# A ring of weight slots in a decoder trunk: three slots with separate low halves, or four with the low half over the raw weights

## The chip, the cores and the metric

One NeuronCore of a Trainium2 chip. The metric is the device time of one launch in microseconds, the median of several runs. Engines: TensorE (PE in the profile) multiplies, VectorE (DVE) and ScalarE (ACT) work on tiles in on-chip memory (SBUF) or in the accumulator banks (PSUM), GpSimd (POOL) does a little elementwise work, and SyncE (SP) issues the DMAs. Each engine runs its own instructions in order; semaphores tie them together.

## The reference

Two decoder layers on 512 tokens of width 1024, all in float32. Cut to what matters here:

```python
for i in range(2):
    p = h @ w_in[i]                       # in0: 22 column tiles of 128, in1: 29
    mix = mixers(p) @ w_out[i]            # RWKV-7 and RG-LRU in layer 0, Conformer conv and Mamba-2 in layer 1
    h = layer_norm(alpha * h + mix)
    q, k, v = h @ wq[i], mem @ wk[i], mem @ wv[i]   # mem has 256 tokens
    h = layer_norm(alpha * h + softmax(q @ k.T / 16) @ v @ wo[i])
    h = layer_norm(alpha * h + square(relu(h @ w1[i])) @ w2[i])   # 4096 hidden
```

All the weight matrices come from HBM once: 263 chunks of 128 x 1024 floats (512 KB).

## The kernel before, in words

**Three products for one.** A float32 product is made of three passes: each operand is split into a rounded high half and the rest, its low half. `mm3` (L525) multiplies activation low by weight high (L527), high by low (L528), high by high (L529); for token-major stages the operands change sides, so L527 holds the weight's low half. A chunk is 24 multiplies of 512 columns in most stages, 24 of 256 columns in the `k` stages, 12 of 512 in the `v` stages.

**The ring of weight slots.** Chunk c uses slot c mod `W_SLOTS` (3) of three arrays: `w_raw`, `w_hi`, `w_lo`. SyncE loads `w_raw` (L339), after `w_split >= c - 2`, that is, when VectorE has made the low half of chunk c-3. ScalarE's `split` (L1055) waits for the landing and for `chunk_done >= c - 2` (TensorE is through with chunk c-3), and copies `w_raw` to `w_hi` (L1063). VectorE's `split` (L1506) waits for that and subtracts into `w_lo` (L1512), which counts up `w_split`. TensorE waits for `w_split >= c + 1` before it starts chunk c, and counts up `chunk_done` at its end.

**Where the splits stand.** The splits are written into the instruction order of ScalarE and VectorE by hand. In a loop over the chunks of a stage both call `chunk(stage, i)`: split up to chunk c + `W_SLOTS` - 1, then wait for `chunk_done` of c, then do the work on chunk c's output. `ahead` does the same without that last wait. So when chunk c-1 is done, both engines split chunk c+2 and only then turn to what follows. Between stages stand calls such as `split(FIRST["out0"] + 2 + W_SLOTS)` (L1231, L1775) before the mixer's output is turned back to features (L1234), `split(FIRST["wo0"] + W_SLOTS)` (L1289, L1891) before the softmax (`row_max`, `probs`), and those in `ln_std` (L1240) and `residual` (L1819) inside the LayerNorms after `out0` and `out1`.

**Stages, in order, per layer l.** `in` (22 or 29 chunks), the mixer, `out` (8 or 12), `k`, transposes of h to features (`to_features`, L952), `v`, `q`, attention, `wo`, transposes, four times `up` and `down` (8 chunks each), transposes. `out`, `v`, `wo` and `down` run in two halves of output columns; the last chunk (or two, `by_token`) of a half goes token tile by token tile, and VectorE's `residual` adds each tile to h. In `in0` and `in1` the vector work of the mixers is woven into the chunk loop; `in1` has 77 filter taps (L1528) on VectorE, beside sums on GpSimd. SyncE's order also has x (`h`, 2 MB) behind a wait at chunk `out0`+2, six loads of LayerNorm rows (`gb`, 1 MB) and two of mem (1 MB).

Of the kernel before, what the change touches and what calls it, by code (L numbers as in the profile page):

```python
# [14 lines left out]
F32R = mybir.dt.float32r  # L15
# [4 lines left out]
P = 128  # L20
# [4 lines left out]
MEM = 256  # L25
HALF = 512
CHUNK = 1024
W_SLOTS = 3
PAD = 4
PW = PAD + T  # L30
ALPHA = 4.0 ** 0.25
# [30 lines left out]
FIRST = {}  # L62
# [78 lines left out]
def build(nc, x_tok, x_feat, mem_feat, weights, vectors, lora, lru_w, ln_rows, out):  # L141
    with ExitStack() as ctx:
        base = (nc.sbuf_base + 31) // 32 * 32
        place = {"at": base}

        def sb(name, shape, dt=F32, at=None):

            size = 4
            for n in shape[1:]:
                size *= n  # L150
            if at is None:
                at = place["at"]
                place["at"] = at + (size + 31) // 32 * 32
            return nc.alloc_sbuf_tensor_at(name, shape, dt, offset=at)

        w_raw = sb("w_raw", [P, W_SLOTS, CHUNK])
        w_hi = sb("w_hi", [P, W_SLOTS, CHUNK], F32R)
        w_lo = sb("w_lo", [P, W_SLOTS, CHUNK], F32R)
        h_at = place["at"]
        h = sb("h", [P, NT, D])  # L160
        act_at = place["at"]
# [126 lines left out]
        def S(name):  # L288
            if name not in sems:
                sems[name] = ctx.enter_context(nc.semaphore(name))  # L290
            return sems[name]
# [19 lines left out]

        landed = [S(f"w_landed{i}") for i in range(W_SLOTS)]
        block = ctx.enter_context(nc.Block())
# [10 lines left out]
        @block.sync  # L324
        def _(sp):
            sp.dma_start(stage[:, 0:2], x_feat[:, 0:2]).then_inc(S("x_in0"), 16)
            sp.dma_start(w_raw[:, 0], weights[0]).then_inc(landed[0], 16)
            for i in range(1, 4):
                sp.dma_start(stage[:, 2 * i:2 * i + 2], x_feat[:, 2 * i:2 * i + 2]).then_inc(S(f"x_in{i}"), 16)
            sp.dma_start(w_raw[:, 1], weights[1]).then_inc(landed[1], 16)  # L330
            sp.dma_start(vec[:], vectors).then_inc(S("vec_in"), 16)
            sp.dma_start(lora_sb[:], lora).then_inc(S("const_in"), 16)
            sp.dma_start(lru_sb[:], lru_w).then_inc(S("const_in"), 16)
            ln_at = {FIRST["out0"] + 6: 0, FIRST["up0_0"] + 2: 1, FIRST["down0_3"] + 1: 2,
                     FIRST["out1"] + 3: 3, FIRST["up1_0"] + 2: 4, FIRST["down1_3"] + 1: 5}
            for c in range(2, N_CHUNKS):
                if c >= W_SLOTS:
                    sp.wait_ge(S("w_split"), c - W_SLOTS + 1)
                sp.dma_start(w_raw[:, c % W_SLOTS], weights[c]).then_inc(landed[c % W_SLOTS], 16)  # L339
                if c == FIRST["out0"] + 2:  # L340
                    sp.wait_ge(S("rst_mm"), 2 * NRC - 2)
                    sp.dma_start(h[:], x_tok).then_inc(S("h_in"), 16)
                if c in ln_at:
                    n = ln_at[c]
                    if n == 0:
                        sp.wait_ge(S("mix_done"), 1)
                    if n:
                        sp.wait_ge(S("h_ready"), NT * n)
                    if n == 3:
                        sp.wait_ge(S("s_bc"), 4)  # L350
                        sp.wait_ge(S("s_conv"), 8)
                    sp.dma_start(gb[:], ln_rows[n:n + 1].to_broadcast([P, 2, D])).then_inc(S("gb_in"), 16)
                for l in range(2):
                    if c == FIRST[f"out{l}"] + 6:
                        sp.wait_ge(S("mix_done"), l + 1)
                        sp.dma_start(stage[:].rearrange("p a t -> p (a t)")[:, 0:8 * MEM], mem_feat)\
                            .then_inc(S("mem_in"), 16)
            for t in range(NT):
                sp.wait_ge(S("out_rows"), t + 1)
                sp.dma_start(out[:, t], h[:, t]).then_inc(S("stored"), 16)  # L360
            sp.wait_ge(S("stored"), 16 * NT)
# [1877 lines left out]
```

## Time and profile before

| | |
|---|---|
| median of 3 runs | 1891.06 us (1889.82 to 1892.39) |
| the profiled execution | 1890.95 us, of it 1889.2 from the first to the last instruction |
| mean granted clock of TensorE | 0.942 |
| busy: TensorE, VectorE, ScalarE, GpSimd | 1718.4, 1127.0, 748.6, 214.2 us |
| the chain that ended last | TensorE 72%, VectorE 20%, ScalarE 4% |
| DMA | 155.53 MB, mean 82 GB/s |

How to read it: the times are one execution's. A busy TensorE is not one at its peak, since multiplies overlap; a 512-column multiply shows 0.39 us and the next starts 0.23 us later. The timeline gives, for each instruction, its start and length, and in brackets how long its engine sat idle before it and whose end released it. Where two rows of one engine are merged, the count follows the x.

### The profile page before, as it was taken

What the parts mean: (1) busy time and instruction counts of PE and PEld (TensorE: products, weight loads), DVE (VectorE), ACT (ScalarE), POOL (GpSimd) and SP (SyncE); (2) the same over time, 40 slices, a digit from 0 to 9 for tenths busy, and PEclk for the clock granted to TensorE, in tenths of its full rate; (3) what the DMA queues carried; (4) which work ended last, traced back from release to release, by engine and by line L of the source; (5) the groups of instructions that cost most, each with busy time, mean ns of one, the idle gap of its engine ahead of it and who ended that gap; (6) DMA issues with size and microseconds to landing.
All of it is one profiled execution on the core that took longest, in us unless ns stands there. A gap on an engine that the chain in (4) does not pass through costs nothing.

```text
span 1889.2 us, 26635 instructions
## 1 busy us (share of the span) xinstructions
PE 1718.4 (91%) x10894; PEld 1420.7 (75%) x10894; DVE 1127.0 (60%) x1377; ACT 748.6 (40%) x995; POOL 214.2 (11%) x186
## 2 busy tenths in 40 slices
PE   7996999889899999999996876789898999999997
PEld 6775899687777888888785664458887778888885
DVE  3689462555656543434559987886555665434345
ACT  4553431345425232324335554553454252324131
POOL 5112300000000000000006833440000000000000
PEclk9997995899999999999998888889998999999999
DMA  5220000444113333333231222003441223333331
GB/s 183 78 73 17 3 5 8 160 123 134 56 62 94 102 90 101 91 102 120 78 96 40 66 67 89 1 1 112 123 134 57 78 78 101 93 102 96 101 120 59
DMA packets 40873, 155.53 MB, mean 82 GB/s; under 512 B 4528, under 2 KB 4656, under 8 KB 39600
## 3 DMA queue, kind: packets, MB, share of 16 engines
q1 hardware_dynamic: 40752, 153.83, 26.4%
q8 instruction: 86, 1.41, 0.3%
q14 instruction: 35, 0.29, 0.1%
HBM read 151.72 MB, written 2.10 MB: 81 GB/s over the span
## 4 chain that ended last, share of the span: by engine, by line
PE 72%; DVE 20%; ACT 4%; issue 2%; DMA 0%; SPq 0%; POOL 0%; DVEq 0%; ACTq 0%; POOLq 0%
PE bank L527 21%; PE bank L528 21%; PE bank L529 21%; DVE cacc L1528 4%; DVE w_lo L1512 3%; DVE p L1525 1%; DVE sconv L1528 1%; DVE h L1528 1%; PE bank L685 1%; DVE nbh L1573 1%; ACT w_hi L1063 1%; PE bank L655 1%; PE bank L704 1%; PE bank L698 1%; DVE lnst L1834 1%
## 5 line engine op out<-in xcount | busy, mean ns | idle before, releaser
L1512 DVE TENSOR_TENSOR w_lo<-w_raw,w_hi 128x1024 fp32r<-128x1024 f32 x263 | 335.2, 1275 | 307.3 <-ACT w_hi L1063 304.7
L527 PE MATMUL bank<-act_lo,w_hi 128*128 128x512 f32 x1048 | 421.5, 402 | 55.7 <-DVE w_lo L1512 47.4
L1063 ACT ACTIVATE w_hi<-w_raw 128x1024 fp32r<-128x1024 f32 x263 | 279.0, 1061 | 367.7 <-PE bank L529 355.7
L528 PE MATMUL bank<-act_hi,w_lo 128*128 128x512 f32 x1048 | 416.7, 398 | 0.0
L529 PE MATMUL bank<-act_hi,w_hi 128*128 128x512 f32 x1048 | 415.7, 397 | 0.0
L527 PEld LDWEIGHTS bank<-act_lo,w_hi 128*128 128x128 f32 x1048 | 202.4, 193 | 107.2 <-issue 49.3
L529 PEld LDWEIGHTS bank<-act_hi,w_hi 128*128 128x128 f32 x1048 | 202.1, 193 | 43.6
L528 PEld LDWEIGHTS bank<-act_hi,w_lo 128*128 128x128 f32 x1048 | 202.7, 193 | 42.6 <-issue 0.7
L527 PE MATMUL bank<-w_lo,aux_hi 128*128 128x512 f32 x576 | 224.5, 390 | 5.3 <-DVE act_lo L1525 5.3
L528 PE MATMUL bank<-w_hi,aux_lo 128*128 128x512 f32 x576 | 224.1, 389 | 0.0
L529 PE MATMUL bank<-w_hi,aux_hi 128*128 128x512 f32 x576 | 224.1, 389 | 0.0
L484 POOL TENSOR_TENSOR cacc<-cacc,gtmp 128x512 f32<-128x512 f32 x44 | 73.5, 1671 | 664.6 <-ACT gtmp L1350 661.7
L527 PEld LDWEIGHTS bank<-w_lo,aux_hi 128*128 128x128 f32 x576 | 108.1, 188 | 28.9 <-DVE act_lo L1525 5.7
L527 PE MATMUL bank<-w_lo,act_hi 128*128 128x512 f32 x288 | 115.7, 402 | 12.8 <-DVE act_lo L1525 10.4
L529 PEld LDWEIGHTS bank<-w_hi,aux_hi 128*128 128x128 f32 x576 | 108.1, 188 | 22.5
L528 PEld LDWEIGHTS bank<-w_hi,aux_lo 128*128 128x128 f32 x576 | 108.1, 188 | 22.3
L528 PE MATMUL bank<-w_hi,act_lo 128*128 128x512 f32 x288 | 114.3, 397 | 0.0
L529 PE MATMUL bank<-w_hi,act_hi 128*128 128x512 f32 x288 | 114.2, 396 | 0.0
L1525 DVE TENSOR_TENSOR stage<-stage 128x512 f32<-128x512 f32 x64 | 44.3, 692 | 108.4 <-ACT stage L1321 108.4
L1321 ACT ACTIVATE stage<-bank 128x512 f32<-128x512 f32 x64 | 38.2, 597 | 146.1 <-PE bank L529 146.1
L1528 DVE SCALAR_TENSOR_TENSOR cacc<-cu,vec,cacc 128x512 f32<-128x512 f32 x75 | 91.7, 1278 | 0.0
L1525 DVE TENSOR_TENSOR aux_lo<-stage,aux_hi 128x512 fp32r<-128x512 f32 (+1 forms) x66 | 48.9, 741 | 59.8 <-ACT aux_hi L1323 53.7
(356 smaller groups left out, 2365.0 us busy)
## 6 DMA issues: line engine op xcount, KB each, us to landing
w_raw<-weights SPq DMA_DIRECT2D x263, 512.0 KB, 3.6
gb<-ln_rows SPq DMA_DIRECT2D x6, 1024.0 KB, 5.7
stage<-x_feat SPq DMA_DIRECT2D x4, 512.0 KB, 6.2
h<-x_tok SPq DMA_DIRECT2D x1, 2048.0 KB, 8.1
stage<-mem_feat SPq DMA_DIRECT2D x2, 1024.0 KB, 5.7
out<-h SPq DMA_DIRECT2D x4, 512.0 KB, 2.6
lora_sb<-lora SPq DMA_DIRECT2D x1, 512.0 KB, 8.8
lru_sb<-lru_w SPq DMA_DIRECT2D x1, 512.0 KB, 9.6
```

Source lines behind the costliest of these rows:

```text
L484: pool.tensor_tensor(acc, acc, gtmp[:, n % 2], ALU.add).then_inc(S("c_conv3"), 1)
L527: pe.matmul(o, whi, xlo, start=first, stop=False)
L528: pe.matmul(o, wlo, xhi, start=False, stop=False)
L529: return pe.matmul(o, whi, xhi, start=False, stop=last)
L655: last = pe.matmul(o[rows_(c), split_cols(j, c)], lhs[feat, j, cf], rhs[feat, j, cf], start=True, stop=True)
L685: last = each(lambda c, q, tok, feat, cf, ct: pe.matmul(compact(o, j, c, q, n), M_[b][tok, j, ct], halves(XT_[b][tok, j, ct], n, False), s ...
L698: last = each(lambda c, q, tok, feat, cf, ct: pe.matmul(compact(o, j, c, q, n), y_[tok, j, ct], halves(x_[tok, j, ct], n, True), start=Tru ...
L1063: act.activation(w_hi[:, s], w_raw[:, s], ACT.Copy).then_inc(S("w_hi_done"), 1)
L1321: done(act.activation(stage[:, n % 2], bank(f"up{l}_{q}", i)[:], ACT.Relu), "up_out")
L1512: dve.tensor_tensor(w_lo[:, s], w_raw[:, s], f(w_hi[:, s]), ALU.subtract).then_inc(S("w_split"), 1)
L1525: return dve.tensor_tensor(o, a, b_, op)
L1528: return dve.scalar_tensor_tensor(out=o, in0=a, scalar=s, in1=b_, op0=op0, op1=op1)
```

## The change

The low half of a chunk is written over its raw weights: `w_lo` gets the address of `w_raw`. The memory saved gives a fourth slot. The raw load of chunk c now waits for `chunk_done >= c - 3`, the end of TensorE's work on chunk c-4, since TensorE reads the low half from there; before, it waited for a split. `W_SLOTS` also stands in all the calls above, so each asks for one chunk more. The load of x keeps its place right behind the last chunk of that sort (`out0`+3 now).

```diff
--- before.py
+++ after.py
@@ -25,7 +25,7 @@
 MEM = 256
 HALF = 512
 CHUNK = 1024
-W_SLOTS = 3
+W_SLOTS = 4
 PAD = 4
 PW = PAD + T
 ALPHA = 4.0 ** 0.25
@@ -153,9 +153,10 @@
                 place["at"] = at + (size + 31) // 32 * 32
             return nc.alloc_sbuf_tensor_at(name, shape, dt, offset=at)
 
+        raw_at = place["at"]
         w_raw = sb("w_raw", [P, W_SLOTS, CHUNK])
+        w_lo = sb("w_lo", [P, W_SLOTS, CHUNK], F32R, at=raw_at)
         w_hi = sb("w_hi", [P, W_SLOTS, CHUNK], F32R)
-        w_lo = sb("w_lo", [P, W_SLOTS, CHUNK], F32R)
         h_at = place["at"]
         h = sb("h", [P, NT, D])
         act_at = place["at"]
@@ -335,9 +336,9 @@
                      FIRST["out1"] + 3: 3, FIRST["up1_0"] + 2: 4, FIRST["down1_3"] + 1: 5}
             for c in range(2, N_CHUNKS):
                 if c >= W_SLOTS:
-                    sp.wait_ge(S("w_split"), c - W_SLOTS + 1)
+                    sp.wait_ge(S("chunk_done"), c - W_SLOTS + 1)
                 sp.dma_start(w_raw[:, c % W_SLOTS], weights[c]).then_inc(landed[c % W_SLOTS], 16)
-                if c == FIRST["out0"] + 2:
+                if c == FIRST["out0"] + W_SLOTS - 1:
                     sp.wait_ge(S("rst_mm"), 2 * NRC - 2)
                     sp.dma_start(h[:], x_tok).then_inc(S("h_in"), 16)
                 if c in ln_at:
```

## Rows read from the trace of the kernel before

**Rows 1.** The page's groups: line, engine, count, then busy us, mean ns, idle before.
```profile
L1512 DVE TENSOR_TENSOR w_lo<-w_raw,w_hi 128x1024 fp32r<-128x1024 f32 x263 | 335.2, 1275 | 307.3 <-ACT w_hi L1063 304.7
...
L1063 ACT ACTIVATE w_hi<-w_raw 128x1024 fp32r<-128x1024 f32 x263 | 279.0, 1061 | 367.7 <-PE bank L529 355.7
```

**Rows 2.** VectorE timeline, in1: start us, us, what, [idle before].
```profile
982.86 1.23 DVE L1512 TENSOR_TENSOR w_lo<-w_raw,w_hi 128x1024 fp32r<-128x1024 f32 x1 [3.08 <-ACT w_hi L1063]
...
988.30 1.23 DVE L1512 TENSOR_TENSOR w_lo<-w_raw,w_hi 128x1024 fp32r<-128x1024 f32 x1 [3.08 <-ACT w_hi L1063]
```

**Rows 3.** Waits of TensorE, window 930 to 1170 (in1).
```profile
PE bank L527 <- DVE w_lo L1512: 32.4, 8, 7.9
```

**Rows 4.** Waits of TensorE, window 20 to 175 (in0).
```profile
PE bank L527 <- DVE w_lo L1512: 3.9, 4, 1.5
```

**Rows 5.** Windows view, in1: length, then busy PE, PEld, DVE, ACT, POOL, clock.
```profile
1002.00:1025.00 23.00, 13.69 (x52) 10.54 (x51) 23.00 (x17) 11.95 (x16) 17.77 (x11) 0.85 0.16 46
```

**Rows 6.** Waits of VectorE, window 976 to 1170.
```profile
DVE w_lo L1512 <- ACT w_hi L1063: 19.7, 5, 6.2
```

**Rows 7.** The page's DMA issues: count, KB each, median us from issue to landing.
```profile
w_raw<-weights SPq DMA_DIRECT2D x263, 512.0 KB, 3.6
```

**Rows 8.** Timeline of ScalarE at the end of k0.
```profile
418.17 0.38 ACT L1076 ACTIVATE k_hi<-bank 128x256 fp32r<-128x256 f32 x1 [1.40 <-PE bank L529]
...
421.05 0.38 ACT L1076 ACTIVATE k_hi<-bank 128x256 fp32r<-128x256 f32 x1 [1.41 <-PE bank L529]
```

**Rows 9.** Timeline of VectorE in in0.
```profile
83.59 1.23 DVE L1512 TENSOR_TENSOR w_lo<-w_raw,w_hi 128x1024 fp32r<-128x1024 f32 x1 [8.80 <-ACT w_hi L1063]
...
119.08 1.22 DVE L1512 TENSOR_TENSOR w_lo<-w_raw,w_hi 128x1024 fp32r<-128x1024 f32 x1 [4.89 <-ACT w_hi L1063]
```

**Rows 10.** Timeline of ScalarE in out0.
```profile
346.25 1.06 ACT L1063 ACTIVATE w_hi<-w_raw 128x1024 fp32r<-128x1024 f32 x1 [4.36 <-PE bank L529]
...
347.22 3.19 ACT L1234 ACTIVATE p<-bank,vec 128x512 f32<-128x512 f32 x4
```

**Rows 11.** Timeline of TensorE in out0.
```profile
352.22 0.77 PE L527 MATMUL bank<-w_lo,act_hi 128*128 128x512 f32 x1 [4.32 <-DVE act_lo L1525]
```

**Rows 12.** Windows view, 352 to 356; granted clock after the busy times.
```profile
352.00:356.00 4.00, 3.78 (x9) 3.03 (x10) 3.80 (x7) 0.90 (x3) 0.00 (x0) 0.50 0.00 0
```

**Rows 13.** Timeline of VectorE at the end of out0's first half.
```profile
361.96 1.23 DVE L1512 TENSOR_TENSOR w_lo<-w_raw,w_hi 128x1024 fp32r<-128x1024 f32 x1 [4.54 <-ACT w_hi L1063]
...
363.10 0.68 DVE L1528 SCALAR_TENSOR_TENSOR h<-h,bank 128x512 f32<-128x512 f32 x1
```

**Rows 14.** Timeline of TensorE in k0, then in k1.
```profile
404.90 0.35 PE L527 MATMUL bank<-aux_lo,w_hi 128*128 128x256 f32 x1 [4.45 <-DVE w_lo L1512]
...
1346.94 0.35 PE L527 MATMUL bank<-aux_lo,w_hi 128*128 128x256 f32 x1 [2.26 <-DVE w_lo L1512]
```

**Rows 15.** TensorE timeline, end of k0 (L963 transposes h).
```profile
422.02 2.95 PE L963 MATMUL bank<-ident,h 128*128 128x128 f32 x25 [0.24 <-DVE k_lo L1525]
```

**Rows 16.** Raw loads issued from 405 to 425, tile w_raw.
```profile
DMA to landing us min/median/max: 3.6/4.0/4.5
```

**Rows 17.** Timeline of ScalarE after q0.
```profile
494.13 1.06 ACT L1063 ACTIVATE w_hi<-w_raw 128x1024 fp32r<-128x1024 f32 x1
```

**Rows 18.** Timeline of VectorE after q0 (softmax).
```profile
496.69 0.69 DVE L1895 TENSOR_REDUCE small<-bank 128x2 f32<-128x512 f32 x1 [0.17 <-PE bank L529]
...
498.19 0.69 DVE L1895 TENSOR_REDUCE small<-bank 128x2 f32<-128x512 f32 x1 [0.61 <-PE bank L529]
```

**Rows 19.** Timeline of VectorE at the LayerNorm after wo0.
```profile
565.45 1.23 DVE L1512 TENSOR_TENSOR w_lo<-w_raw,w_hi 128x1024 fp32r<-128x1024 f32 x1 [3.23 <-ACT w_hi L1063]
...
566.93 0.69 DVE L1528 SCALAR_TENSOR_TENSOR h<-h,bank 128x512 f32<-128x512 f32 x1 [0.25 <-PE bank L529]
...
575.16 0.69 DVE L1528 SCALAR_TENSOR_TENSOR h<-h,bank 128x512 f32<-128x512 f32 x1 [0.67 <-PE bank L529]
...
577.05 0.16 DVE L1528 SCALAR_TENSOR_TENSOR lnmv<-lnmv,lnsd 128x1 f32<-128x1 f32 x1
```

## The prediction

> **What bounds the kernel now.** I read the page's groups first, then the waits by engine and by window, then the timelines at each place where TensorE stops. TensorE is the bound in most stages: splitting a chunk costs ScalarE 1.06 and VectorE 1.2 us [rows 1], and a 512-column chunk takes TensorE 5.44 us (VectorE's two splits in [rows 2] each follow a chunk's end and are 5.44 apart; that is 24 multiplies, one each 0.23 us). So in `q`, `wo`, `up` and `down` the ring of three slots is no limit. TensorE is held up by the weight split for 32.4 us in `in1` [rows 3] and for 3.9 in `in0` [rows 4]. That looks like the prize of a fourth slot, but in `in1` VectorE is busy for all 23 us of a 23 us window while TensorE works 13.7 [rows 5]. VectorE waits 19.7 us between 976 and 1170 [rows 6], and three of its five waits (3.08 us each [rows 2] shows one) come before the filter taps start. What is behind the stage is VectorE's own work; TensorE's stalls are what it leaves over.
>
> **The change part by part.** In steady state the new rule is harmless. The end of chunk c-1 now issues the raw load of chunk c+3. It lands 3.6 us later [rows 7], then come 1.06 and 1.23 us of splitting, with some 0.15 us of signals: the split stands 6.05 us after that end, and TensorE wants it 3 x 5.44 = 16.3 us after it (3 x 2.88 = 8.6 in `k`, by the two chunk ends in [rows 8]). The old split stood 2.5 us after the end, because its raw data lay there long before. The price is elsewhere: ScalarE and VectorE are in order and the split stands at a fixed place in their programs. Whatever follows it starts up to 3.65 us later, if the split came right after a chunk's end. In the loops of `up`, `q` and `down` nothing hangs on that: both engines finish the split at 6.05 us, the next output comes at 5.44, and the lag of 0.6 us stays inside the slack before `down` reads it. I take 0 there. If that cover failed, each of the 64 `up` chunks could cost 0.6. The serial places remain:
>
> 1. `in0`: TensorE stalls four times for a split, 3.9 us [rows 4]. VectorE's waits of 8.80 and 4.89 us [rows 9] end when ScalarE has its gate values, which come out of TensorE after chunks 9 and 15, both stalled for some 1.1 us. Splits one chunk ahead free both: -2.2. The first loads are not late: chunk 4's now waits for chunk 0, but is needed three chunks later.
>
> 2. `out0`, before the mixer's output goes back: ScalarE splits `out0`+4 right at the end of `out0`+1 (346.25) and only then turns the mixer rows back (347.22) [rows 10], and TensorE waits for their low halves until 352.22 [rows 11]. Now it must split `out0`+5, whose load starts at that same end. +3.7 (3.6 and 0.1 of signals), nothing hides it.
>
> 3. `out0`, end of the first half: VectorE splits at 361.96, then adds the four tiles from 363.10 [rows 13], and the second half needs the banks they free. The split now ends 3.5 later. +3.5.
>
> 4. `k0`, `k1`: TensorE waits 4.45 us for chunk `k0`+3 and 2.26 for `k1`+3 [rows 14], because that split stands behind the LayerNorm in both programs. With four slots the one that stands there is +4, wanted 2.88 us later; but the split inside `residual` waits for a load that the last `out` chunk releases. In layer 0 the split of mem already covers most of the first such wait, so the LayerNorm ends 1.4 later: 4.45 + 1.4 - 2.9 = 2.95, -1.5. In layer 1 nothing covers it, 3.5 later: +0.6.
>
> 5. End of `k` (2 times): chunk `k0`+7 ends at 421.0 [rows 8] and the transposes go on at 422.02, held by the last low half of k by 0.24 [rows 15]. Before that low half now stands the split of `v0`+2, whose load waits for the end of `k0`+6. Loads here take 4.0 [rows 16]: 4.0 + 1.06 + 1.23 + 0.42 + 0.2 after that end is 4.0 after the end of `k0`+7 against 1.0 now. +3.0 each, 6.0.
>
> 6. Softmax (2 times): the split of `wo0`+2 (494.13) [rows 17] stands before the loop over score tiles; VectorE starts it with waits of only 0.17 and 0.61 us for TensorE [rows 18] and then sets its pace, and TensorE waits at its end. The split of `wo0`+3 needs a load released by the last `q` chunk: 3.1 later, less those two waits and some overlap, +2.4 each, 4.8.
>
> 7. LayerNorm after `wo0`, `down0_3`, `wo1` (3 times): the last split before it starts at 565.45, the first tile at 566.93, 0.25 after it was free to; the last tile comes at 575.16 and takes until 577.2 [rows 19]. Starting 3.2 later at 2.05 us a tile against TensorE's 2.72, VectorE is 0.7 behind at the last tile: +0.65 each, 2.0. The split of `up`+1, which now stands earlier, lies beside the transposes, so its move gains 0. After `down1_3` no chunk is left to load: 0.
>
> 8. `in1`: at chunk 8 VectorE splits at 988.30 [rows 2] and then begins the taps that fill it to the end. Its split now waits for the load that chunk 7's end releases. ScalarE's copy of chunk 7 (some 0.65 us) stood before the split and now runs beside the load: 3.65 - 0.65 = +3.0. Later waits for the split hang on VectorE's own earlier steps (ScalarE's dt chain, the dt transposes), so they stay. Bounds: from -10 (the last two waits of [rows 6] go) to +6.
>
> Writing over its own input is free for VectorE: `h<-h,bank` does it in 0.68 for 512 columns [rows 13], half of the 1.23 of a 1024-column split; no row shows the new form, so bounds of 0 and 0.1 us, hidden except in `in1`. SyncE issues in order: behind a raw load that waits for TensorE now stand x, the LayerNorm rows and mem, all needed over 15 us later: 0.
>
> Sum: -2.2 + 3.7 + 3.5 - 1.5 + 0.6 + 6.0 + 4.8 + 2.0 + 3.0 = +19.9. Against the profiled execution's 1890.95 us that is 1910.9, and that execution stands at the median (1891.06). I say 1911.
>
> The trace's landing of 3.6 us can be put beside a rule of the Trainium skill ("SBUF — State Buffer", The DMA setup-cost knee): a transfer costs about 2 us whatever its size, plus its bytes at 436 GB/s. By that 512 KB would be an estimated 3.2 us, 0.4 less at each of some ten exposed loads, and the sum about 16. The measured 3.6 decides.
>
> **The rivals.**
> - *The prize is real.* If TensorE's stalls in `in1` set the stage's end, through ScalarE waiting for chunk ends, a fourth slot gives back up to 32.4 us [rows 3]: 1910.9 - 3.0 - 32.4 = 1875.5. It decides from 23 us on (19.9 + 3.0); below that the kernel is slower still. Against it: VectorE's full window [rows 5]. The Trainium skill ("Perfetto Trace Analysis", Optimization Strategy) says that equal gaps repeating on the engine that should be full can mean too few buffers, which is this rival.
> - *The waits are absorbed.* If the softmax loop, the end of `k`, the LayerNorms and `in1` catch up before TensorE needs them, items 5 to 8 fall away and -2.2 + 3.7 + 3.5 - 1.5 + 0.6 = +4.1 stays: 1895. For it: the transposes wait only 0.24 for VectorE [rows 15]; against it: VectorE has 0.17 and 0.61 us of slack [rows 18].
> - *The clock goes on top.* After the 4.32 us wait in `out0` the granted clock is 0.50 [rows 12] and the first multiply takes 0.77 us [rows 11], where the ring's others start each 0.23. Seven stops get longer by 2.4 to 3.7 us. If each brings one more us at 1.2 GHz: 1918; the bound is twice that, 1925.
> - *It doesn't do what it says.* If the fourth slot buys no lead because the load waits for TensorE, items 1 and 4 gain nothing: -2.2 and -1.5 fall away and `k` loses 3.5 in each layer: 1920.
>
> **How the numbers follow.** Forecast 1911 (1903 to 1917) 0.60; the clock on top 0.14; absorbed in part or whole 0.11, of it 0.04 within 0.2% (3.8 us, about what a measurement of this kernel can tell from no change); no lead 0.08; the prize 0.07, of it 0.01 within 0.2%. Leaving out the prize and the ends of the others, the range is 1900 to 1922. Faster 0.06, same 0.05, slower 0.89.
>
> **What would show it.** `w_raw` issues right after chunk ends instead of after splits; ScalarE's waits before `w_hi` end with a landing. In `out0`, 3.7 us more between the end of `out0`+1 and the next multiply, and 3.5 more before the second half. After `k`, a wait of 3 us on `k_lo`. The first score tile 2.4 us later against the last `q` chunk. TensorE's waits for `w_lo` in `in1` fall well below 32.4 while the stage gets no shorter. The prediction is wrong if `in1` shortens by over 10 us, or if the softmax and `k` stops don't lengthen.

## The result and the profile after

| | before | changed kernel |
|---|---|---|
| median | 1890.94 us (16 runs) | 1911.92 us (16 runs) |
| ratio of the times | | 1.0108 (95%: 1.0083 to 1.0132) |
| profiled execution, of it first to last instruction | 1890.95, 1889.2 | 1914.34, 1912.6 |
| mean granted clock | 0.942 | 0.937 |

The change makes the kernel slower by 21.0 us in the medians and by 23.4 in the profiled executions. The forecast was +19.9 and 1911 us. Line numbers of the changed kernel are those of before plus one.

The page of the changed kernel: busy times, the chain that ended last, the two split groups and the first multiply (columns as in [rows 1]), and the load.

```profile
PE 1731.3 (91%) x10894; PEld 1430.4 (75%) x10894; DVE 1123.7 (59%) x1377; ACT 745.3 (39%) x995; POOL 214.0 (11%) x186
...
PE bank L528 20%; PE bank L530 20%; PE bank L529 20%; DVE cacc L1529 3%; DMA w_raw<-weights 3%; DVE w_lo L1513 2%; DVE p L1526 2%; DVE sconv L1529 1%; DVE h L1529 1%; ACT w_hi L1064 1%; DVE lnst L1835 1%; PE bank L686 1%; DVE act_lo L1526 1%; PE bank L656 1%; PE bank L705 1%
...
L1513 DVE TENSOR_TENSOR w_lo<-w_raw,w_hi 128x1024 fp32r<-128x1024 f32 x263 | 328.6, 1251 | 521.0 <-ACT w_hi L1064 514.1
L1064 ACT ACTIVATE w_hi<-w_raw 128x1024 fp32r<-128x1024 f32 x263 | 278.5, 1060 | 616.9 <-DMA w_raw<-weights 586.7
L528 PE MATMUL bank<-act_lo,w_hi 128*128 128x512 f32 x1048 | 421.0, 402 | 43.2 <-DVE w_lo L1513 37.3
...
w_raw<-weights SPq DMA_DIRECT2D x263, 512.0 KB, 3.6
```

The two splits cost what they cost before, and the load lands in the same 3.6 us. What is new is who releases them. In [rows 1] ScalarE's idle time before `w_hi` was ended by TensorE. Here 586.7 of 616.9 us end with the landing of a raw load, and the load has entered the chain that ended last, with 3%. VectorE, the next in line, waits 514 us for ScalarE ahead of `w_lo`. Most of this is idle time that costs nothing; the places where it does are serial.

The first is in `out0`. ScalarE, VectorE and TensorE (timelines: start, length, what, idle before):

```profile
350.15 1.06 ACT L1064 ACTIVATE w_hi<-w_raw 128x1024 fp32r<-128x1024 f32 x1 [4.16 <-DMA w_raw<-weights]
351.12 3.19 ACT L1235 ACTIVATE p<-bank,vec 128x512 f32<-128x512 f32 x4
```
```profile
356.12 0.77 PE L528 MATMUL bank<-w_lo,act_hi 128*128 128x512 f32 x1 [7.79 <-DVE act_lo L1526]
```
```profile
369.12 1.23 DVE L1513 TENSOR_TENSOR w_lo<-w_raw,w_hi 128x1024 fp32r<-128x1024 f32 x1 [7.82 <-ACT w_hi L1064]
370.27 0.68 DVE L1529 SCALAR_TENSOR_TENSOR h<-h,bank 128x512 f32<-128x512 f32 x1
```

In [rows 10] ScalarE split at 346.25, right behind `out0`+1, and turned the mixer rows at 347.22. Here `out0`+1 ends 0.4 us later than before, the split stands 3.9 later, the mixer rows behind it too, and TensorE's wait of 4.32 [rows 11] has become 7.79. At the end of the first half the split of 361.96 [rows 13] stands at 369.12, 3.6 us later than the first stop alone explains, and the four sums behind it wait with it.

The second place is the end of `k0` (chunk `k0`+7 ends at 428.13). VectorE and TensorE, and TensorE's first multiply of `v0` in the kernel before (whose `k0`+7 ends at 421.03):

```profile
427.20 1.23 DVE L1513 TENSOR_TENSOR w_lo<-w_raw,w_hi 128x1024 fp32r<-128x1024 f32 x1 [1.18 <-ACT w_hi L1064]
428.35 0.42 DVE L1526 TENSOR_TENSOR k_lo<-bank,k_hi 128x256 fp32r<-128x256 f32 x1
429.97 1.23 DVE L1513 TENSOR_TENSOR w_lo<-w_raw,w_hi 128x1024 fp32r<-128x1024 f32 x1 [1.21 <-ACT w_hi L1064]
431.11 0.42 DVE L1526 TENSOR_TENSOR k_lo<-bank,k_hi 128x256 fp32r<-128x256 f32 x1
```
```profile
431.58 4.62 PE L964 MATMUL bank<-ident,h 128*128 128x128 f32 x25 [2.44 <-DVE k_lo L1526]
438.15 0.47 PE L528 MATMUL bank<-w_lo,aux_hi 128*128 128x512 f32 x1 [1.95 <-DVE act_lo L1526]
```
```profile
427.62 0.47 PE L527 MATMUL bank<-w_lo,aux_hi 128*128 128x512 f32 x1 [2.65 <-DVE act_lo L1525]
```

The last low half of k stands behind a split whose load was released by `k0`+6: the transposes wait 2.44 us where they waited 0.24 [rows 15]. The granted clock then falls. The stretch from the end of `k0`+7 to that of `v0`+0, by windows (columns as in [rows 5]), here and in the kernel before:

```profile
428.13:442.50 14.37, 9.94 (x45) 8.27 (x44) 5.61 (x8) 4.72 (x6) 0.00 (x0) 0.78 0.13 38
```
```profile
421.00:430.60 9.60, 6.71 (x46) 5.78 (x44) 3.84 (x5) 3.77 (x5) 0.00 (x0) 1.00 0.28 68
```

What the lower clock costs stands in the rows: the 25 transposes take 4.62 us where they took 2.95 [rows 15], and chunk `v0`+0, from its first multiply to its end at 442.51, takes 4.36 where it took 2.99 (427.62 to 430.61). That is 3.0 us together.

### The profile page after: what moved, and what is told of

Its sections match the earlier page's. It is cut to its first block, busy times and chain, and to the rows that moved or that the text cites. A ratio compares the mean times of both kernels' runs of the same rounds, so it can differ in the third digit from the quotient of the medians.

```text
span 1912.6 us, 26637 instructions
## 1 busy us (share of the span) xinstructions
PE 1731.3 (91%) x10894; PEld 1430.4 (75%) x10894; DVE 1123.7 (59%) x1377; ACT 745.3 (39%) x995; POOL 214.0 (11%) x186
## 4 chain that ended last, share of the span: by engine, by line
PE 71%; DVE 19%; ACT 4%; issue 3%; DMA 3%; SPq 0%; POOL 0%; DVEq 0%; ACTq 0%; POOLq 0%
PE bank L528 20%; PE bank L530 20%; PE bank L529 20%; DVE cacc L1529 3%; DMA w_raw<-weights 3%; DVE w_lo L1513 2%; DVE p L1526 2%; DVE sconv L1529 1%; DVE h L1529 1%; ACT w_hi L1064 1%; DVE lnst L1835 1%; PE bank L686 1%; DVE act_lo L1526 1%; PE bank L656 1%; PE bank L705 1%
## 5 line engine op out<-in xcount | busy, mean ns | idle before, releaser
L1513 DVE TENSOR_TENSOR w_lo<-w_raw,w_hi 128x1024 fp32r<-128x1024 f32 x263 | 328.6, 1251 | 521.0 <-ACT w_hi L1064 514.1
L1064 ACT ACTIVATE w_hi<-w_raw 128x1024 fp32r<-128x1024 f32 x263 | 278.5, 1060 | 616.9 <-DMA w_raw<-weights 586.7
L528 PE MATMUL bank<-w_lo,act_hi 128*128 128x512 f32 x288 | 116.3, 404 | 19.9 <-DVE act_lo L1526 13.9
L528 PEld LDWEIGHTS bank<-w_lo,act_hi 128*128 128x128 f32 x288 | 55.7, 193 | 33.7 <-issue 11.7
L529 PEld LDWEIGHTS bank<-w_hi,act_lo 128*128 128x128 f32 x288 | 55.8, 194 | 12.1 <-issue 0.5
```

The source lines that it names most:

```text
L528: pe.matmul(o, whi, xlo, start=first, stop=False)
L529: pe.matmul(o, wlo, xhi, start=False, stop=False)
L1064: act.activation(w_hi[:, s], w_raw[:, s], ACT.Copy).then_inc(S("w_hi_done"), 1)
L1513: dve.tensor_tensor(w_lo[:, s], w_raw[:, s], f(w_hi[:, s]), ALU.subtract).then_inc(S("w_split"), 1)
```

## The experiments

Times are medians, each ratio is to runs of the kernel before on the same chip. "Shift" is the end of a chunk in one profiled execution less that in another. The first four ran together, with the kernel before at 1890.02 us.

**1. Split three chunks ahead, all else as changed** (both engines; every such call).

```diff
+LOOK = 3
-                split(c + W_SLOTS)
+                split(c + LOOK)
...
-            split(FIRST["out0"] + 2 + W_SLOTS)
+            split(FIRST["out0"] + 2 + LOOK)
```

> Four slots in place and the new rule for the raw load, but ScalarE and VectorE split only three chunks ahead, at the places where the kernel before splits. Theory (the price is the landing that stands between the end of a chunk and the split): the raw load of a chunk is now issued one whole chunk before its split, 5.44 us for a 512-column chunk against a landing of 3.6, so nothing is exposed but some 0.8 us in k, where a chunk is 2.88. The time goes back to 1891 us (1888 to 1895). Rival (writing the low half in place, or SyncE waiting for TensorE, costs by itself): it stays at 1905 or above. In out0 the stretch from the end of out0+1 to that of out0+2 shrinks by about 3 us against the changed kernel.

Measured: 1889.57 us, ratio 1.0001 (0.9979 to 1.0023). The loss is gone, with the in-place write, the fourth slot and the new rule all still there. From `out0`+1 to `out0`+2 are 12.4 us (17.5 changed, 14.4 before). ScalarE's waits before `w_hi` for the load, in this kernel and in the changed one (us in total, times, longest):

```profile
ACT w_hi L1065 <- PE bank L531: 343.9, 82, 7.1
ACT w_hi L1065 <- DMA w_raw<-weights: 13.0, 12, 5.3
```
```profile
ACT w_hi L1064 <- DMA w_raw<-weights: 586.7, 191, 12.9
```

The landing ended 191 waits; with one chunk between the load's issue and its split it ends 12. So the price of the change is the distance between load and split. With that chunk between, the in-place write, the fourth slot and the new rule cost nothing that this interval (some 4 us either way) can show.

**2 and 3. The new rule alone, three slots; then the same with the low halves in place.**

```diff
 # 2: the kernel before
-                    sp.wait_ge(S("w_split"), c - W_SLOTS + 1)
+                    sp.wait_ge(S("chunk_done"), c - W_SLOTS + 1)
 # 3: the changed kernel
-W_SLOTS = 4
+W_SLOTS = 3
```

> The kernel before with one line changed: the raw load of chunk c waits for the end of chunk c-3 in place of the split of c-3; three slots, low halves in their own buffer. Theory: every exposed landing of the changed kernel is there and the gains of the fourth slot are not: -2.2 and -1.5 fall away and k loses 3.5 in each layer, so 1911.9 + 2.2 + 1.5 - 0.6 + 7.0, about 1922 us (1916 to 1930). Rival (the loss comes from writing in place or from the fourth slot's order of work): it stays within 5 us of 1891.

> As rule_only_3_slots, and the low halves are written over the raw weights. The two differ by the in-place write alone. Theory: in place costs VectorE nothing, the two are within 2 us of each other and w_lo is 1.23 us each in both. Rival: writing over the input costs up to 0.1 us for each of 263 splits, or serialises them, and this one is more than 3 us slower than its pair.

Measured: 1937.83 us (1.0258, 1.0234 to 1.0281) and 1939.0 us (1.0251, 1.0216 to 1.0286). In place is free, as expected: 1.2 us apart, and each split takes the same time in both:

```profile
L1512 DVE TENSOR_TENSOR w_lo<-w_raw,w_hi 128x1024 fp32r<-128x1024 f32 x263 | 333.4, 1268 | 539.2 <-ACT w_hi L1063 537.2
```
```profile
L1513 DVE TENSOR_TENSOR w_lo<-w_raw,w_hi 128x1024 fp32r<-128x1024 f32 x263 | 331.3, 1260 | 541.7 <-ACT w_hi L1064 539.6
```

The size was missed: 47.8 us where I expected 32. By the shifts the extra lies in the short chunks. From the end of `k` to that of `v` the rule alone loses 8.5 and 7.7 us in the two layers (4.7 and 3.2 changed). Most of it is the stop ahead of `v`, 6.1 and 5.7 us (4.8 and 3.4 changed); inside `v` it loses 2.4 and 2.0, in stalls of some 1 us at every third chunk. `q` and its start lose another 1.8 and 2.3, where the changed kernel loses 0. A chunk of `v` is 2.72 us, so two chunks ahead is 5.44 us, less than the 6.05 us of load and split. The fourth slot hides that inside `v`.

**4. Three ahead only where a serial step follows**

```diff
+def look(stg, i):
+    return 3 if stg == "out0" or (stg in ("k0", "k1") and i > 5) or (stg, i) == ("in1", 8) else 4
-                split(c + W_SLOTS)
+                split(c + look(stg, i))
...
-            split(FIRST["out0"] + 2 + W_SLOTS)
+            split(FIRST["out0"] + 2 + look("out0", 2))
...
-                split(FIRST[f"wo{l}"] + W_SLOTS)
+                split(FIRST[f"wo{l}"] + 3)
```

> The changed kernel with the split three chunks ahead only where a serial step stands right behind it: in out0, at k+6 and k+7 of both layers, ahead of the softmax of both layers, and at in1+8; four ahead elsewhere. Theory: of the shifts read in the changed kernel's trace, those of out0 (3.2 and 5.0), the end of k (4.8 and 3.4), the softmax (2.2 and 1.3) and in1 (2.8), 22.7 in sum, go; what stays is in0 +0.4, k -1.4 and +0.3, the LayerNorms +1.8. That gives 1911.9 - 22.7, about 1889 us, or 1890 to 1894 if some of these are not additive. Rival (the price is spread over every split, also in the ring of up, down, q): it stays above 1900.

Measured: 1892.53 us (1.001, 0.9991 to 1.0028), some 19 us of the 21 back. By stages, against the kernel before: from the end of `in0` to that of `out0` -0.3 (+8.5 changed), `k0` -1.9, `v0` +1.3, `wo0` +0.9, `in1` with `out1` -0.4 (+2.4 changed), `v1` +1.4, `wo1` +1.2. So the stops that I had listed carry nearly all of the price, and the ring of `up`, `q` and `down` none.

**5 and 6. One stop at a time** (with 7 and 8, the kernel before at 1890.69 us): three ahead only at `k`+6 and `k`+7; then only at `q`+7 and ahead of the softmax.

```diff
 # 5
+    return 3 if (stg in ("k0", "k1") and i > 5) else 4
 # 6
+    return 3 if stg in ("q0", "q1") and i == 7 else 4
-                split(FIRST[f"wo{l}"] + W_SLOTS)
+                split(FIRST[f"wo{l}"] + 3)
```

> The changed kernel with the split only three chunks ahead at k+6 and k+7 of both layers, nothing else. Theory: the stop after k, 4.79 and 3.39 us in the changed kernel's trace, falls to the 1.30 and 1.41 that look4_where_not_serial still showed there, so -5.5: 1906.5 us (1904 to 1909), with the stages before it unchanged. Rival (removing one stop only moves it to v): v0 and v1 keep their +4.7 and the time stays at 1911.

> The changed kernel with the split three chunks ahead at q+7 and at the split ahead of the softmax, in both layers, nothing else. Theory: the shifts of the wo stage against the kernel before, +2.2 in layer 0 and +1.3 in layer 1, go to within 0.4 of zero: -3.0, 1909 us (1907 to 1911). In look4_where_not_serial, which kept q+7 at four, +0.9 and +1.2 stayed; if they stay here too, the split at q+7 was not their cause.

Measured: 1907.47 us (1.0102, 1.0068 to 1.0136) and 1908.05 us (1.0103, 1.0064 to 1.0142), 4.5 and 3.9 less than the changed kernel. Both intervals hold the changed kernel's ratio of 1.0108, so the times alone show no gain; it is the traces that place it. At the end of `k0` the stretch that took 14.37 takes 9.6 us again, at the clock of 1.00:

```profile
423.40:433.00 9.60, 6.71 (x45) 5.75 (x44) 5.27 (x7) 4.72 (x6) 0.00 (x0) 1.00 0.20 58
```

In layer 1 it takes 10.8 (13.0 changed, 9.6 before). Ahead of the softmax the shift of `wo` falls from +2.2 and +1.3 to -0.8 and 0.0, more than in kernel 4, which had left the split at `q`+7 where it was. In layer 0 one of these 3 us comes back between `wo0` and `up0_0`: that stretch is +1.2 here and +0.2 in the changed kernel. So the softmax stop is worth some 2 us in layer 0.

**7 and 8. A later load**, in the changed kernel and in the one before:

```diff
+                if c >= 8:
+                    sp.dma_start(dly[:], vectors[:, 0:2]).then_inc(S("dly_in"), 16)
+                    sp.wait_ge(S("dly_in"), 16 * (c - 7))
                 sp.dma_start(w_raw[:, c % W_SLOTS], weights[c]).then_inc(landed[c % W_SLOTS], 16)
```

> The changed kernel, with SyncE loading 8 bytes to each partition and waiting for them ahead of every raw weight load from chunk 8 on. That puts one small load's landing (some 2 us, an estimate from half the big one's 3.6) between the end of a chunk and the issue of the next raw load. Theory: the price is paid at each serial place, so each of them grows by these 2 us: out0 twice, end of k twice, softmax twice, in1, the first part of k twice, the LayerNorms by some 0.7 each: 9 x 2 + 2, about +20, 1932 us (1924 to 1945). Rival (the loss is not the landing): within 4 us of 1912.

> The same small load ahead of every raw load, in the kernel before. Its raw loads are issued when the split of the chunk three back is done, some 10 us ahead of their own split, so 2 us more should cost nothing: 1891 (1889 to 1894). If it costs over 5 us, the small load itself disturbs something, and its pair has to be read less that much.

Measured: 1944.18 us (1.0294, 1.023 to 1.0359) and 1904.96 us (1.0085, 1.0053 to 1.0118). The second expectation fell: the small load isn't harmless. Alone it lands in 1.6 us, but behind a raw load in `k0` SyncE waits 3.3 to 3.6 us for it, and in `v` and `q` it adds up (+6.7 and +3.4 us in layer 0). SyncE in the kernel before with the small load, at a chunk of `up` and at the end of `k0`:

```profile
602.67 0.33 SPq L341 DMA_DIRECT2D dly<-vectors  x1
604.24 0.33 SPq L343 DMA_DIRECT2D w_raw<-weights  x1
```
```profile
419.34 0.53 SPq L341 DMA_DIRECT2D dly<-vectors  x1
422.67 0.33 SPq L343 DMA_DIRECT2D w_raw<-weights  x1
```

Read less its pair, as said beforehand, the delay costs the changed kernel 32.3 - 14.3 = 18.0 us, against some 20 expected. That number isn't worth much: kernel 7's four runs are 1932.94, 1935.7, 1952.66 and 1954.93 us, and the median stands between two groups. The traces from the end of `out0`+0 on, which leave out the scan where the clock differs (below), give 42.8 us for the changed kernel and 20.5 for the one before, so 22.3. In `out0` the two stops grow by 1.7 and 1.0 us. That fits a price that follows the landing, but the pair is too coarse to show more.

**9 and 10. Where `in0`'s gain went.** VectorE loses time beside GpSimd there (below), so GpSimd's two gelu steps were moved; 9 is kernel 1 with that, 10 splits four ahead in `in0` alone. These, 11 and 12 look for a better kernel too.

```diff
             pool.wait_ge(S("l_gact"), 1)
-            gelu(pool.tensor_scalar(li[:], li[:], 0.044715, 1.0, ALU.mult, ALU.add))
-            gelu(pool.tensor_tensor(li[:], li[:], g_, ALU.mult))
...
             clear(yt_(0, 2), 0)
+            pool.wait_ge(*made("rw", 1))
+            gelu(pool.tensor_scalar(li[:], li[:], 0.044715, 1.0, ALU.mult, ALU.add))
+            gelu(pool.tensor_tensor(li[:], li[:], g_, ALU.mult))
```

> look3_all with GpSimd's two gelu steps (2.1 and 5.3 us, at 153.6 to 161.6) moved behind the first two tiles of the rw products, to about 185, where they stand beside TensorE's and VectorE's work on banks. In the kernel before VectorE is held up beside them: nbh 2.81 and w_lo 5.40 us in place of 1.22 each, and TensorE waits 17.0 us for VectorE there. Theory: these 5.8 us of VectorE come back, TensorE's wait falls to about 11 and the end of in0 to the first scan product is 5 to 6 us shorter: 1885 us (1883 to 1889). Rival (the chain through GpSimd, ScalarE's tanh and the lc products becomes late, or the collision moves to VectorE's products at 189 to 196): within 2 us of 1890 or slower.

> As look3_gelu_later, but the splits stand four chunks ahead in in0 (three elsewhere). It tells where the gain of 2.2 us that I had forecast for in0 went. Theory: VectorE was 1.86 us ahead until it met GpSimd's step, where it lost half of it; with that step gone the lead reaches the next stage, and TensorE's first product behind in0 comes 1.9 us earlier than in look3_gelu_later, both read from the end of in0_1+3. Rival (the lead is lost on TensorE, whose chunk 16 and 17 came 2.1 us late): less than 1 us between the two.

Measured: 1885.17 us (0.9968, 0.9947 to 0.9989) and 1880.56 us (0.9938, 0.9907 to 0.9968), the kernel before at 1890.01. The end of TensorE's wait for `m`, in the kernel before, the changed one, 9 and 10:

```profile
174.35 3.32 PE L655 MATMUL bank<-p,kh 64*64 64x64 f32 x64 [17.03 <-DVE m L1669]
```
```profile
173.43 3.32 PE L656 MATMUL bank<-p,kh 64*64 64x64 f32 x64 [14.75 <-DVE m L1670]
```
```profile
167.59 3.32 PE L658 MATMUL bank<-p,kh 64*64 64x64 f32 x64 [9.92 <-DVE m L1672]
```
```profile
162.55 3.32 PE L661 MATMUL bank<-p,kh 64*64 64x64 f32 x64 [9.95 <-DVE m L1675]
```

Kernel 10 is 5.04 us ahead of 9 here; 1.68 of it is a first load that landed earlier (the shift at `in0_1`+3), which leaves 3.4, more than the 1.9 expected: 2.2 is VectorE's lead behind its wait at chunk 15, and 1.1 comes from one split less in the stretch ahead of `m`. So the fourth slot has a gain in `in0`. In the changed kernel it is lost on the way.

**11 and 12. The wait ahead of the scan**, filled with multiplies whose result nothing uses, in the kernel before and in kernel 10:

```diff
                     pe.wait_ge(*out_sem(f"rat{b}", 2))
+                    if b:
+                        idle = take("rst0", 0)
+                        for _ in range(10):
+                            pe.matmul(idle[:, 0:P], ident[:], ident[:], start=True, stop=True)
                     pe.wait_ge(*out_sem(f"rrho{b}", 2))
```

> The kernel before, with ten 128x128 multiplies of the identity matrix into a free bank ahead of TensorE's last wait before the scan products. They compute nothing that is used; they fill a wait of 1.27 us at 279. In nine of the ten profiled executions so far the granted clock falls from 1.00 to 0.50 at that wait and stays low until some 330; in one it stayed at 1.00, and the stretch took 169.7 us in place of 190. Theory: it is that wait which lets the clock fall; filled, it stays at 1.00 and the time goes to about 1870 us. Rival (the clock falls for what runs before or after it, 64-column multiplies in a row): it falls within some us anyway and the time stays within 2 us of 1891.

> in0_look4_gelu_later with the ten filling multiplies of filled_gap_before. Theory: the two gains add, since one lies before the scan and the other in it: 1880.6 - 19.5 = 1861 us (1858 to 1865), with the granted clock at 1.00 through the scan. Rival (with the stretch ahead some 10 us shorter, the clock falls at another place, or has fallen before the filled gap): 1875 or above, and the clock at 0.50 somewhere between 262 and 330.

Measured: 1870.47 us (0.9899, 0.9875 to 0.9924), and 1859.35 us (0.9847, 0.9808 to 0.9886; the kernel before at 1890.94). TensorE's wait, then the windows of the kernel before (the clock is the third number from the end), then those of kernel 11:

```profile
280.41 0.29 PE L763 MATMUL bank<-p 64*64 64x64 f32 x2 [1.27 <-DVE p L1525]
```
```profile
280.00:300.00 20.00, 19.48 (x295) 19.13 (x296) 1.87 (x5) 1.15 (x3) 0.00 (x0) 0.57 0.01 2
300.00:330.00 30.00, 29.71 (x398) 28.47 (x396) 9.46 (x24) 4.56 (x11) 0.00 (x0) 0.50 0.05 10
```
```profile
280.00:300.00 20.00, 19.77 (x484) 19.10 (x484) 5.33 (x14) 2.76 (x7) 0.00 (x0) 1.00 0.01 4
300.00:330.00 30.00, 25.51 (x286) 20.64 (x283) 16.57 (x33) 13.75 (x23) 0.00 (x0) 1.00 0.39 141
```

Both theories held: the clock stays at 1.00 where it had fallen (in kernel 12 it is 1.00 from 262 to 300 and 0.94 from there to 330), and the time follows. Kernel 12 is faster than either kernel of the comparison, and by 31.6 us than the one before. Of that 21.2 are the clock (1880.56 to 1859.35), some 5 GpSimd's step (1890.01 to 1885.17), and 4.6 the fourth slot used in `in0` alone (1885.17 to 1880.56). The intervals of 9 and 10 still overlap.

## Why the prediction was right or wrong

Each term against its shift in the changed kernel's trace:

| step | predicted | measured | with the split three ahead there |
|---|---|---|---|
| 1 `in0` (with the mixer, to `out0`+0) | -2.2 | +0.4 | |
| 2 `out0`+1 to +2 | +3.7 | +3.2 | -0.7 (kernel 4) |
| 3 end of the first half of `out0` | +3.5 | +4.9 | +0.1 (kernel 4) |
| 4 `k0`, `k1` | -1.5, +0.6 | -1.4, +0.3 | |
| 5 end of `k` | +3.0, +3.0 | +4.8, +3.4 | 0.0, +1.2 (kernel 5) |
| 6 softmax | +2.4, +2.4 | +2.2, +1.3 | -0.8, 0.0 (kernel 6) |
| 7 LayerNorms | +0.65 three times | +0.2, -0.4, +1.9 | |
| 8 `in1` | +3.0 | +2.8 | -0.5 (kernel 4) |

The measured terms and -0.2 in `v1` add up to the 23.4 us of the profiled executions. The mechanism was right, and kernels 1 and 4 to 6 show it by taking it away; the sum hides two errors. That the median (1911.92) came within 1 us of the forecast is in part luck: of the terms above, those set too low are off by 7.6 us together and those set too high, with `v1`, by 4.0, and the profiled executions stand 3.5 us above the forecast sum. The changed kernel's runs spread, too: two of the 16 took 1889.18 and 1891.7 us.

**Step 1 failed.** The premise held: TensorE's stalls at chunks 9, 14 and 15 went, and chunk 15 ended 3.27 us earlier. VectorE's wait that ended at 119.08 [rows 9] ended at 117.22, 1.86 earlier, and it was still 1.7 ahead at 154. What I left out is what stands behind it.

TensorE lost its own lead at once. Behind chunk 15 it reached the low-rank products (L626) early, waited 0.94 us, and the granted clock fell; here is that multiply, and the stretch in the changed kernel and in the one before:

```profile
109.23 4.99 PE L626 MATMUL bank<-p,lora_sb 64*128 64x512 f32 x8 [0.94 <-DVE p L1526]
```
```profile
108.00:120.00 12.00, 11.06 (x27) 6.19 (x25) 7.67 (x8) 6.74 (x8) 0.00 (x0) 0.72 0.13 44
```
```profile
108.00:120.00 12.00, 12.00 (x50) 8.70 (x49) 6.97 (x7) 6.95 (x10) 0.00 (x0) 1.00 0.36 108
```

Chunk 16 ended 13.71 us after chunk 15, where it had been 8.34, and TensorE ended `in0` no earlier (150.97 against 150.93). In kernel 10 TensorE waited 0.93 us at the same place, but the clock stayed at 1.00, chunk 16 took 10.45, and VectorE's lead over kernel 9 was 2.2, the figure forecast. So some 0.4 of the forecast may have gone here, by one pair of traces.

VectorE lost its lead beside GpSimd. VectorE in the changed kernel, and the same step in the one before:

```profile
154.01 2.80 DVE L1513 TENSOR_TENSOR w_lo<-w_raw,w_hi 128x1024 fp32r<-128x1024 f32 x1
156.73 5.53 DVE L1526 TENSOR_TENSOR p<-p,prb 128x1024 f32<-128x1024 f32 x1
```
```profile
157.29 5.40 DVE L1512 TENSOR_TENSOR w_lo<-w_raw,w_hi 128x1024 fp32r<-128x1024 f32 x1
162.61 1.21 DVE L1525 TENSOR_TENSOR p<-p,prb 128x1024 f32<-128x1024 f32 x1
```

GpSimd works on 2048 columns twice here, the second time for 5.36 us from 155.81 (5.34 from 156.26 before). In both kernels the VectorE operation that stood beside this one ended 1.09 us after it, at 162.26 and 162.69, so being early bought little: the lead became 0.93. Moving GpSimd's step away (kernels 9 and 10) brought the lead through. The 0.93, and 0.4 more, went at the scan, where the clock fell earlier, on multiplies that then run at half speed (windows 278:282: 1.00 before, 0.63 changed). That part is read from the trace; but the stretch from `in0_7`+3 to `out0`+0 takes 187.3 to 192.2 us among executions of like code, so one pair of traces can't show it, and I leave it at that.

**Steps 3 and 5 were mis-sized**, by +1.4 and +1.8 (layer 0). I had priced the wait and left the clock to a rival at 14%. At the end of `k0` the transposes went on 2.5 us later, less than the 3.0 forecast; the lower clock then took 3.0 us in the transposes and the first `v` chunk, and 0.7 came back, since TensorE's next wait was 1.95 in place of 2.65. In step 3 the granted clock was 0.76 over the 14.4 us that end with `out0`+4, where it had been 0.82 over 9.6. If what lies under 1.00 is time at 0.50, half of that time is lost: by this estimate 3.5 us in place of 1.7. The clock rival was right at these two stops, and its price of 1 to 2 us each fits them; at all seven it would have given more than was measured. Step 6 was 1.1 too high in layer 1.

**Step 7 looks small through the clock.** At the three stops the granted clock was 0.91, 0.83 and 0.91 before, and 1.00, 1.00 and 0.84 in the changed kernel, so the clock makes the first two shifts look smaller and the third larger. In kernel 5, which leaves these stops as changed and had 0.92 at all three, they are +1.2, +0.7 and +2.1. The term of 0.65 was low: VectorE took the last tile of `wo0` 1.00 us and that of `wo1` 1.74 us after the chunk's end, where it had been 0.09. Kernel 6 has +1.2, +0.9 and +0.5; why the third hangs on the split at the softmax stays open.

**Steps 2, 4 and 8 held**, with their reasons: the stall of `k0` moved from `k0`+3 to `k0`+4 and shrank by the 1.4 us. In `in1` the split ahead of the taps carries the whole price, and kernel 4, with that one moved back, has none. What the prediction said would be seen there was only half seen: TensorE's waits for `w_lo` fell from 32.4 [rows 3] to 26.2 us, while VectorE went on working without a gap:

```profile
PE bank L528 <- DVE w_lo L1513: 26.2, 8, 6.2
PE bank L884 <- DVE stm L2024: 14.0, 1, 14.0
```
```profile
1019.00:1042.00 23.00, 16.12 (x62) 12.52 (x60) 23.00 (x14) 14.04 (x19) 21.98 (x14) 0.85 0.21 60
```

TensorE waits as often for the split (8 times in both), less in sum, and then 14.0 us for `stm`, where it waited 7.6. That refutes the rival of the prize (1875.5 us); what decided was the window in which VectorE, which feeds TensorE, is full. The Trainium skill ("Perfetto Trace Analysis", Optimization Strategy) says that such equal gaps can mean too few buffers; in `in1` they did not. The break-even of that rival was mis-added: a gain of 19.9 - 3.0 = 16.9 us would have been enough, not 23. The landing is 3.6 us again by the page of the profile, not the estimated 3.2 worked out from the Trainium skill ("SBUF — State Buffer", The DMA setup-cost knee).

"It doesn't do what it says" is refuted for the same stages, since the stalls at chunks 14 and 15 and at `k0`+3 did go. Experiments 2 and 3 show what would have been left without the fourth slot's lead: 1938 us, not the 1920 of that rival (its own terms add up to 1921), which had no term for `v` and too little for the stop ahead of it.

## What to carry to other kernels

A slot that is refilled when TensorE ends with it has its data one landing later; on engines that run in order, a split placed at that same chunk end pays that landing at every serial step behind it, 21 us here, and one chunk between the load's issue and its split takes it all away. So set the number of slots and the distance of the split apart: more slots give lead to the load, and only where the stage itself gains (here `in0`) to the split. Before counting a gain on one engine, look at what it runs into next: an operation of GpSimd, or a clock that falls, can take it back.

## What the runs showed of the hardware

- Two VectorE operations of 1.22 us took 2.80 and 5.53 beside two of GpSimd over 2048 columns (2.10 and 5.36). GpSimd's same steps beside TensorE's products and VectorE's work on banks (kernel 9: 1.90 and 4.54 us from 179 on) cost the kernel nothing that shows: 1885.17 against 1889.57.
- A load of 8 bytes to each partition landed in 1.6 us alone and in 3.3 to 3.6 behind one of 512 KB (kernel 8, `k0`).
- The granted clock can hang on a wait of 1.27 us. In the kernel before it falls right behind it (1.00 in 278:282, 0.58 in 282:286) and the scan runs at 0.50 until some 330; with the wait filled it stays at 1.00, and the kernel is 19.5 us faster (1890.01 to 1870.47). The wait alone doesn't decide: in kernel 7's profiled execution TensorE waited 1.28 us at the same place, the clock stayed at 1.00, and `in0_7`+3 to `out0`+0 took 169.7 us, as in kernel 11 (169.9). Single runs that are some 20 us shorter, of the kernel before (1865.95) and of the changed one (1889.18), may be the same; no profile of one was taken.
